# Product-key experts of a two-layer encoder step on one core: decode tokens by row gathers, dense stages 512 columns wide, sums kept in PSUM, low parts subtracted on VectorE

## The chip, the cores and the metric

One Trainium2 chip, one of its NeuronCores. The metric is device microseconds of one execution, the median of a few runs. The kernel before takes 5514.44 us (three runs, 5514.37 to 5516.7).

## What is computed

A two-layer encoder trunk over 512 prompt tokens and 32 decode tokens. Each layer is a mixer (RG-LRU and RWKV-7 side by side), then product-key expert retrieval, then a per-layer input embedding. Only the experts (`peer_ffn`) are changed:

```python
# per token: 8 heads, two half-queries each; u, v are (128*128, 1024)
q = (xb @ wq).reshape(PEER_BLOCK, PEER_HEADS, 2, PEER_HALF)
s = jnp.einsum('thsc,hskc->thsk', q, keys)            # 16 rows of 128 scores
top_s, top_i = lax.top_k(s, 16)
cand = top_s[:, :, 0, :, None] + top_s[:, :, 1, None, :]
best_s, best_c = lax.top_k(cand.reshape(PEER_BLOCK, PEER_HEADS, 256), 16)
e = (i1 * N_KEYS + i2).reshape(PEER_BLOCK, 128)       # 128 experts of each token
gate = softmax(best_s)
hid = jnp.einsum('td,tkd->tk', xb, jnp.take(u, e, axis=0))
wgt = gate * gelu(hid)
out = jnp.einsum('tk,tkd->td', wgt, jnp.take(v, e, axis=0))
```

## The kernel before

The program is written in five instruction streams (SyncE for loads, GpSimd, TensorE, ScalarE, VectorE) that meet at semaphores; each stream runs in the order in which it is written. SyncE, ScalarE and GpSimd also issue DMAs, in their own order.

The experts are computed densely: for each of 128 tiles of 128 experts, all 544 tokens are multiplied with all of them, and a gate matrix with zeros for the experts a token did not choose weighs the result. To keep float32 accuracy at the speed of float32r, each operand is cut into a high part (a copy rounded to float32r) and a low part (the rest), and each product is three matmuls (high x high, high x low, low x high).

**Hidden stage** (`hidden`, line 749). For one tile of experts: load 128 x 1024 weights (`load_u`), ScalarE makes the high part (`high_u`, line 1020), GpSimd the low part (`low_u`, line 505), TensorE does 48 matmuls (8 slices x 3 products x 2 halves of 272 tokens), ScalarE applies gelu (line 1027) and stores the result to memory (`expert_inputs`). Tiles go in pairs over two slots.

**Routing** (`route`, VectorE) runs beside it in blocks of 128 tokens, and a fifth of the 32 decode tokens. TensorE makes a block's scores (`scores`, line 759), ScalarE copies them out of PSUM (line 1035), VectorE does two rounds of top-16 (`top16`: lines 1380 to 1390) and the look-up of the numbers (lines 1424 to 1428), TensorE turns the result (`turn`). So far 16 hidden tiles run beside it (`PAIRS_A`); I call this part A of a block. In part B (`PAIRS_B`, 12 tiles), VectorE builds one-hot matrices of 4 tokens at a time (line 1446), GpSimd multiplies one with the gates (`weigh`, line 511), TensorE multiplies them (`gates`, line 780: 4 matmuls of 128 columns), ScalarE copies the product into a staging tile (line 1050). Two such groups follow each hidden tile; eight more groups stand alone at the end of the block. Then ScalarE stores the block's 8 MB of gates (`save`).

**Expert stage** (line 820). In 32 steps of 4 tiles: values and both matrices are loaded, VectorE multiplies gates and gelus (line 1463), makes the high part of the values (line 1458) and the low part of the products (line 1467), ScalarE the high part of the products (line 1095), GpSimd the low part of the values (line 538), TensorE does 24 matmuls of 272 columns for each of 8 output slices, and VectorE adds each slice to the residual `h` (line 1128).

Everything else (mixer, projections, norms, embedding) is the same in both kernels.

## Time and profile before

| | us |
|---|---|
| median of 3 runs | 5514.44 |
| span of the profiled execution | 5514.9 |
| first layer, from the end of the first scores to the end of the hidden stage's hand-over | 797.0 to 1866 |
| first layer, expert stage | 1866 to 2652 |
| second layer, the same two | 3534.3 to 4603, 4603 to 5390 |

TensorE is busy 86% of the span, GpSimd 36%, VectorE 55%, ScalarE 23%. The profiled execution stands within 0.5 us of the median, so sums made against the one hold for the other. In the rows below times are microseconds from the span's start; an arrow in brackets names what the engine had waited for.

### The profile page before, as it was taken

The numbers are of one execution on the slowest core, as the hardware profiler recorded it, in microseconds if no ns is written. First come the engines' busy times: TensorE is split into PE (matmuls) and PEld (weight loads), VectorE is DVE, ScalarE is ACT, GpSimd is POOL, SyncE is SP. The second block draws the span as 40 slices with busy tenths as digits, with TensorE's granted clock in tenths as the row PEclk, the third lists the DMA queues.
The fourth block names the chain that finished last, engine by engine and source line by source line (L and its number), as shares of the span: only waits on it lengthen the run. The fifth ranks groups of instructions, "written<-read, shape, count | busy, mean of one in ns | idle before, by whom it ended". The sixth has DMA issues, their size and how long they took to land.

```text
span 5514.9 us, 102578 instructions
## 1 busy us (share of the span) xinstructions
PE 4748.2 (86%) x38750; PEld 4569.1 (83%) x38750; DVE 3056.5 (55%) x4779; ACT 1254.8 (23%) x1872; POOL 1997.2 (36%) x902
## 2 busy tenths in 40 slices
PE   7566689899898799999884757898998987999997
PEld 7465589899898799999783646898998987999996
DVE  3453325655746577777235541355657456777772
ACT  3321123333332111111123211233333321111101
POOL 4100125463554444444040002363645634444430
PEclk9776899999999899999997768999999998999999
DMA  3000133535435555555120001335344345555541
GB/s 97 26 1 3 43 120 120 156 110 162 150 116 154 152 175 176 174 182 174 56 72 16 1 3 57 127 116 160 122 146 151 118 146 161 183 177 173 177 153 58
DMA packets 488297, 642.85 MB, mean 117 GB/s; under 512 B 60160, under 2 KB 322848, under 8 KB 487200
## 3 DMA queue, kind: packets, MB, share of 16 engines
q1 hardware_dynamic: 286384, 489.77, 27.1%
q10 hardware_dynamic: 201584, 151.55, 8.9%
q8 instruction: 42, 0.69, 0.1%
q0 software_dynamic: 256, 0.59, 0.0%
q14 instruction: 31, 0.25, 0.0%
HBM read 487.47 MB, written 154.35 MB: 116 GB/s over the span
## 4 chain that ended last, share of the span: by engine, by line
issue 43%; PE 36%; POOL 13%; DVE 4%; ACT 2%; DVEq 1%; POOLq 1%; ACTq 0%; DMA 0%; SPq 0%
PE ps L749 12%; PE ps L820 9%; POOL m L538 5%; PE ps L589 5%; POOL m L511 4%; POOL m L505 2%; PE ps L597 2%; PE ps L562 1%; PE ps L780 1%; DVE m L1446 1%; POOL m L485 1%; PE ps L653 1%; PE ps L661 1%; PE ps L698 1%; POOL m L481 1%
## 5 line engine op out<-in xcount | busy, mean ns | idle before, releaser
L749 PE MATMUL ps<-m,m 128*128 128x272 f32 x12288 | 1602.7, 292 | 73.9 <-POOL m L505 48.8
L749 PEld LDWEIGHTS ps<-m,m 128*128 128x128 f32 x12288 | 1578.5, 191 | 79.7 <-issue 79.7
L820 PE MATMUL ps<-m,m 128*128 128x272 f32 x12288 | 1572.1, 290 | 60.9 <-DVE m L1467 56.4
L820 PEld LDWEIGHTS ps<-m,m 128*128 128x128 f32 x12288 | 1558.2, 189 | 74.7 <-DVE m L1467 52.2
L505 POOL TENSOR_TENSOR m<-m,m 128x1024 fp32r<-128x1024 f32 x256 | 673.6, 2632 | 1000.5 <-ACT m L1020 1000.4
L538 POOL TENSOR_TENSOR m<-m,m 128x1024 fp32r<-128x1024 f32 x256 | 689.6, 2703 | 888.3 <-DVE m L1458 888.3
L1446 DVE TENSOR_TENSOR m<-m,m 128x512 f32<-128x512 f32 x544 | 672.2, 1292 | 447.1 <-PE ps L780 247.4
L1128 DVE TENSOR_TENSOR m<-ps,m 128x544 f32<-128x544 f32 (+1 forms) x528 | 378.9, 718 | 453.3 <-PE ps L820 340.4
L1463 DVE TENSOR_TENSOR m<-m,m 128x544 f32<-128x544 f32 x256 | 548.2, 2141 | 72.7 <-DMA m<-expert_inputs 40.9
L589 PE MATMUL ps<-m,m 128*128 128x272 f32 x3648 | 462.0, 289 | 87.3 <-POOL m L485 87.3
L589 PEld LDWEIGHTS ps<-m,m 128*128 128x128 f32 x3648 | 461.3, 191 | 88.9 <-issue 88.9
L1095 ACT ACTIVATE m<-m 128x544 fp32r<-128x544 f32 x256 | 168.8, 659 | 1407.8 <-DVE m L1463 1407.8
L511 POOL TENSOR_TENSOR m<-m,m 128x512 f32<-128x512 f32 x272 | 386.6, 1434 | 93.9 <-DVE m L1446 93.9
L780 PE MATMUL ps<-m,m 128*128 128x128 f32 x2176 | 317.2, 302 | 86.0 <-POOL m L511 85.6
L780 PEld LDWEIGHTS ps<-m,m 128*128 128x128 f32 x2176 | 290.2, 212 | 104.8 <-POOL m L511 104.4
L1027 ACT ACTIVATE m<-ps 128x544 f32<-128x544 f32 x256 | 160.0, 625 | 929.1 <-PE ps L749 827.3
L562 PE MATMUL ps<-m,m 128*128 128x272 f32 x1152 | 273.4, 401 | 77.4 <-DVEq L1364 56.0
L562 PEld LDWEIGHTS ps<-m,m 128*128 128x128 f32 x1152 | 224.2, 195 | 126.7 <-DVEq L1364 56.9
L485 POOL TENSOR_TENSOR m<-m,m 128x1024 fp32r<-128x1024 f32 x76 | 194.9, 2566 | 247.9 <-ACT m L875 247.9
L1020 ACT ACTIVATE m<-m 128x1024 fp32r<-128x1024 f32 x256 | 268.6, 1050 | 1.2 <-ACT m L1004 1.2
L496 POOL DMA_DIRECT2D out_small<-m x2 | 1.3, 649 | 717.0 <-DVEq L1344 717.0
L1380 DVE MAX8 m<-m 128x8 f32<-128x128 f32 (+3 forms) x240 | 59.0, 321 | 344.3 <-ACT m L1035 343.6
(194 smaller groups left out, 3439.2 us busy)
## 6 DMA issues: line engine op xcount, KB each, us to landing
m<-in_ut SPq DMA_DIRECT2D x256, 512.0 KB, 3.3
m<-in_v SPq DMA_DIRECT2D x256, 512.0 KB, 3.7
expert_inputs<-m ACTq DMA_DIRECT2D x256, 272.0 KB, 2.0
m<-gate_matrix SPq DMA_DIRECT2D x256, 272.0 KB, 4.1
m<-expert_inputs SPq DMA_DIRECT2D x256, 272.0 KB, 4.7
gate_matrix<-m ACTq DMA_DIRECT2D x8, 8192.0 KB, 30.5
m<-in_w_in SPq DMA_DIRECT2D x44, 512.0 KB, 3.8
m<-in_wq SPq DMA_DIRECT2D x32, 512.0 KB, 4.1
```

Of the source, the lines that this page charges most:

```text
L505: tt(ul[j], uraw[j], uh[j].bitcast(F32), ALU.subtract).then_inc(ul_ready, 1)
L511: tt(oneB[:, k % 2], oneB[:, k % 2], gate.unsqueeze(2).to_broadcast([P, GT, P]), ALU.mult).then_inc(ab_ready, 1)
L538: tt(vl[half * EC + j], vraw[j % 2], vh[half * EC + j].bitcast(F32), ALU.subtract).then_inc(vl_ready, 1)
L562: last = mm(ps[:, bank + a, 0:HALF], wslot[:, slot, k, :], rhs[:, n, a * HALF:(a + 1) * HALF], start=(n == 0), stop=(n == len(ks) - 1))
L589: last = mm(ps[:, 2 * j + a, 0:HALF], lhs[j][:, k, :], rhs[:, k, a * HALF:(a + 1) * HALF], start=(k + w == 0), stop=(k == KD - 1 and w == 2))
L749: last = mm(ps[:, j * 2 + a, 0:HALF], lhs[j][:, k, :], rhs[:, k, a * HALF:(a + 1) * HALF], start=(k + w == 0), stop=(k == KD - 1 and w == 2))
L780: last = mm(ps[:, 5 + k % 2, j * P:(j + 1) * P], oneA[:, k % 2, j, :], oneB[:, k % 2, j, :], start=True, stop=True)
L820: last = mm(ps[:, 4 + m % 2 * 2 + a, 0:HALF], lhs[at][:, m * P:(m + 1) * P], rhs[at][:, a * HALF:(a + 1) * HALF], start=(j + w == 0), stop ...
L1020: av(uh[j], uraw[j], ACT.Copy).then_inc(uh_ready, 1)
L1128: return tt(cut(at, HALF), halves(bank, HALF), cut(at, HALF), ALU.add)
L1446: tt(hot[:, s], iota.unsqueeze(1).to_broadcast([P, GT, P]), number.unsqueeze(2).to_broadcast([P, GT, P]), ALU.is_equal).then_inc(hot_ready, 1)
L1463: tt(wf[j % 2], gf[j], gs[j], ALU.mult).then_inc(w_ready, 1)
```

## The change

- The 32 decode tokens leave the dense stages. They are routed first, beside the first 8 hidden tiles; GpSimd then gathers, in 64 indirect DMAs a layer, the rows of `u` and `v` of their 128 experts (32 tokens x 4 chosen experts, one row of 1024 on each partition, two buffers). VectorE does the dot products (`dot`) and the weighted sum (`gather_add`), and TensorE folds the four partial sums.
- The dense stages cover 512 tokens: a hidden tile is 24 matmuls of 512 columns instead of 48 of 272.
- In the expert stage the eight output slices stay in the eight PSUM banks over all 128 tiles, and are added to `h` once at the end.
- The weights of both stages go through one ring of four slots (`ring_raw`, `ring_hi`, `ring_lo`); the low part overwrites the raw one. ScalarE makes the high part of both stages (`high`), VectorE the low part (`low`); GpSimd no longer computes in these stages.
- One-hot matrices are made by `tensor_scalar` of 128 x 128, the gate folded in, 16 for a tile. Part A of a block is now 12 hidden tiles, part B 16, each with two gate groups; none stand alone.
- Within routing, `low` is called at points between the steps (`between`).

The core of the diff:

```diff
-PAIRS_A, PAIRS_B = 8, 6
+QUADS_DEC, QUADS_A, QUADS_B = 2, 3, 4
@@ SyncE
+                def load_u(m, j):
+                    sp_.wait_ge(ring_done, L * STEPS + m * RING + j + 1)
+                    sp_.dma_start(ring_raw[j], ut[...]).then_inc(ring_in[j], 16)
@@ GpSimd
-                            weigh(b, g, 2 * j)
-                            weigh(b, g, 2 * j + 1)
-                            low_u(b * PAIRS_N + g + (PAIRS_A + 1), j)
+                for n in range(2 * DOTS):
+                    if n >= ROWS:
+                        pool.wait_ge(row_used, L * (2 * DOTS) + n - ROWS + 1)
+                    pool.indirect_dma_start(rows[n % ROWS], None, (u if n < DOTS else v)..., ...)
@@ TensorE
-                    for a in range(2):
-                        for k in range(KD):
-                            for w, (lhs, rhs) in enumerate([(uh, xh), (uh, xl), (ul, xh)]):
+                    pe.wait_ge(ring_low, i + 1)
+                    pe.wait_ge(ge_out, L * NK + m * RING + j + 1)
+                    for k in range(KD):
+                        for w, (lhs, rhs) in enumerate([(ring_hi, xh), (ring_hi, xl), (ring_lo, xh)]):
+                            last = mm(ps[:, 4 + j % 2, :], lhs[j][:, k, :], rhs[:, k, 0:SEQ], ...)
@@ TensorE, part B
                             hidden(b * QUADS_N + g + (QUADS_DEC + QUADS_A), j)
                             gates(b, g, 2 * j)
                             gates(b, g, 2 * j + 1)
@@ ScalarE
+                def gelu(m, j):
+                    i = L * NK + m * RING + j
+                    act.wait_ge(ring_done, L * STEPS + m * RING + j + 1 + RING)
+                    av(ge[j % 2], ps[:, 4 + j % 2, :], ACT.Gelu_apprx_tanh).then_inc(ge_out, 1)
+                    high(m + (j + RING - 1) // RING, (j + RING - 1) % RING)
+                    act.dma_start(act_d[...], ge[j % 2]).then_inc(act_saved[j % 2], 16)
@@ VectorE
+                def low(m, j):
+                    dve.wait_ge(ring_high, L * STEPS + m * RING + j + 1)
+                    tt(ring_lo[j], ring_raw[j], ring_hi[j].bitcast(F32), ALU.subtract).then_inc(ring_low, 1)
+                def ahead(m, j):
+                    low(m + (j + RING - 1) // RING, (j + RING - 1) % RING)
@@ VectorE, part B
+                        for j in range(RING):
+                            ahead(at + QUADS_A + g, j)
+                            for k in range(2 * j, 2 * j + 2):
+                                dve.wait_ge(gmat_done, i + 1)
+                                for n in range(GT):
+                                    ts(oneB[:, k % 2, n, :], iota, selq[...], selq[...], ALU.is_equal, ALU.mult)
+                                    last = ts(oneA[:, k % 2, n, :], iota, selq[...], None, ALU.is_equal)
+                                last.then_inc(hot_ready, 1)
+                            if j % 2 == 1:
+                                dot(b, g, j // 2)
@@ VectorE, expert stage
+                    for j in range(RING):
+                        weigh(e, j)
+                        low(e + QUADS, j)
+                        low_w(e, j)
```

VectorE in part B, before: one turn of its loop, two gate groups. `m_130` and `m_129` are the two one-hot matrices; after `gmat_done` it waits for nothing.

```order
L1446 ISA [waits gmat_done]
L1446 TENSOR_TENSOR m_130<-m_53,m_117 128x512
L1446 ISA
L1446 TENSOR_TENSOR m_129<-m_53,m_117 128x512
L1443 REGISTER_ALU
L1446 ISA [waits gmat_done]
```

The same place in the change, the first rows of a tile; L1400 is `low`, `m_144` and `m_143` are the one-hot matrices, and `ring_high` is counted up by ScalarE's `high`.

```order
L1399 ISA
L1400 TENSOR_TENSOR m_112<-m_116,m_108 128x1024 [waits ring_high]
L1524 REGISTER_ALU
L1527 TENSOR_SCALAR m_144<-m_53,m_130 128x128 [waits gmat_done]
L1528 TENSOR_SCALAR m_143<-m_53,m_130 128x128
```

The subtraction that stood on GpSimd now stands on VectorE ahead of the one-hot matrices of the same tile.

ScalarE at the same place in the change, one tile: gelu is L1045, `high` of the tile three further on is L1038, the copies of the gate products are L1067.

```order
L1044 ISA [waits ring_done]
L1045 ACTIVATE m_122<-ps 128x512 [waits act_saved0]
L1037 ISA
L1038 ACTIVATE m_111<-m_119 128x1024 [waits ring_in3]
L1047 ISA
L1048 ISA [waits ge_out]
L1048 DMA expert_inputs<-m_122 128x512
L1066 ISA
L1067 ISA [waits gmat_done]
L1067 ACTIVATE m_124<-ps 128x128x4
```

As before, `high` stands behind the gelu of the running tile, which waits for that tile's last matmul (`ring_done`); new is that the rows of VectorE above wait for it.

VectorE in the expert stage of the change, one tile (L1547 gates times gelus, L1400 low part of the values, L1552 low part of the products):

```order
L1547 TENSOR_TENSOR m106_155<-m106_155,m98_147 128x512
L1399 REGISTER_ALU
L1400 TENSOR_TENSOR m64_113<-m68_117,m60_109 128x1024
L1551 REGISTER_ALU
L1552 TENSOR_TENSOR m102_151<-m106_155,m110_159 128x512
```

The additions to `h` and the high part of the values, which stood between such rows before, are gone.

## Rows read from the trace of the kernel before

**Rows 1.** The page, costliest group: xcount | busy us, mean ns | idle before.
```profile
L749 PE MATMUL ps<-m,m 128*128 128x272 f32 x12288 | 1602.7, 292 | 73.9 <-POOL m L505 48.8
```
**Rows 2.** Windows of both stages: length, busy PE, PEld, DVE, ACT, POOL, clock, DMA share, GB/s.
```profile
797.00:1866.00 1069.00, 961.54 (x7387) 948.11 (x7387) 623.35 (x1322) 337.67 (x449) 533.51 (x266) 0.94 0.43 135
1866.00:2652.00 786.00, 782.57 (x6132) 776.24 (x6132) 595.62 (x631) 82.42 (x125) 334.68 (x124) 1.00 0.50 170
```
**Rows 3.** Chain that ended last: start, us, line xcount (f32: two records a matmul).
```profile
1297.05 60.66 PE ps L749 x480
...
5409.08 76.00 PE ps L562 x320
```
**Rows 4.** Timeline, TensorE at the end of part B: start us, us, what.
```profile
1444.98 6.27 PE L749 MATMUL ps<-m,m 128*128 128x272 f32 x48
1451.09 1.95 PE L780 MATMUL ps<-m,m 128*128 128x128 f32 x16
1457.31 3.52 PE L780 MATMUL ps<-m,m 128*128 128x128 f32 x16 [4.26 <-POOL m L511]
```
**Rows 5.** Timeline, part B: from a tile's last matmul to the low part's start.
```profile
1357.79 6.28 PE L749 MATMUL ps<-m,m 128*128 128x272 f32 x48
...
1364.24 0.62 ACT L1027 ACTIVATE m<-ps 128x544 f32<-128x544 f32 x1 [4.54 <-PE ps L749]
...
1364.76 1.05 ACT L1020 ACTIVATE m<-m 128x1024 fp32r<-128x1024 f32 x1
...
1365.88 2.80 POOL L505 TENSOR_TENSOR m<-m,m 128x1024 fp32r<-128x1024 f32 x1
```
**Rows 6.** Timeline of VectorE, one routing of 128 tokens.
```profile
1251.27 3.20 DVE L1380 MAX8 m<-m 128x8 f32<-128x128 f32 x16 [9.36 <-ACT m L1035]
...
1270.88 2.28 DVE L1403 TENSOR_TENSOR m<-m 128x2048 f32<-128x2048 f32 x1
...
1289.19 0.22 DVE L1413 TENSOR_SCALAR m<-m 128x128 uint32<-128x128 uint32 x1
1289.33 0.22 DVE L1414 TENSOR_SCALAR m<-m 128x128 uint32<-128x128 uint32 x1
...
1289.99 2.29 DVE L1424 TENSOR_TENSOR m<-m,m 128x2048 f32<-128x2048 f32 x1
...
1297.08 2.29 DVE L1424 TENSOR_TENSOR m<-m,m 128x2048 f32<-128x2048 f32 x1
```
**Rows 7.** Timeline, expert stage, first step: VectorE with and without GpSimd beside it.
```profile
1853.72 0.72 DVE L1463 TENSOR_TENSOR m<-m,m 128x544 f32<-128x544 f32 x1 [18.44 <-DMA m<-expert_inputs]
...
1863.33 2.35 POOL L538 TENSOR_TENSOR m<-m,m 128x1024 fp32r<-128x1024 f32 x1 [1.90 <-DVE m L1458]
1863.35 2.92 DVE L1463 TENSOR_TENSOR m<-m,m 128x544 f32<-128x544 f32 x1
```
**Rows 8.** Windows of TensorE around a wait of 4.26 us: length, busy, granted clock, DMA, GB/s.
```profile
1456.00:1457.50 1.50, 0.20 (x1) 1.00 0.31 44
1457.50:1459.00 1.50, 1.50 (x9) 0.63 0.79 306
1459.00:1460.50 1.50, 1.50 (x8) 0.50 0.00 0
1460.50:1462.00 1.50, 1.04 (x8) 0.73 0.00 0
```
**Rows 9.** Timeline and waits of ScalarE's queue behind a store of gates.
```profile
1245.82 0.58 ACTq L1055 DMA_DIRECT2D gate_matrix<-m  x1
...
1261.74 10.95 ACTq L1031 DMA_DIRECT2D expert_inputs<-m  x1
```
**Rows 10.** Waits: who for whom, us in total, times, longest.
```profile
ACT m L1027 <- issue: 89.1, 8, 12.5
```
**Rows 11.** DMA issues: KB each, median us to landing.
```profile
m<-expert_inputs SPq DMA_DIRECT2D x256, 272.0 KB, 4.7
gate_matrix<-m ACTq DMA_DIRECT2D x8, 8192.0 KB, 30.5
```

More of the change, by code:

```diff
@@ L441, in _ @@
+                sp_.wait_ge(ring_done, L * STEPS + NK + RING)
+                passed(sp_)
+                for j in range(2, RING):
+                    load_gates(0, j)
+                    load_v(0, j)
                 for j in range(2):
@@ new lines, in _ @@
+                for j in range(RING):
+                    experts(0, j, first=(j == 0))
+                with pe.Fori(1, QUADS - 1) as e:
+                    for j in range(RING):
+                        experts(e, j)
+                for j in range(RING):
+                    experts(QUADS - 1, j, final=(j == RING - 1))
+                pe.wait_ge(bank_added, L + 1)
+                pe.wait_ge(dec_sum, L + 1)
+                passed(pe)
+                for k in range(KD):
+                    last = mm(ps[:, 0, k * DEC:(k + 1) * DEC], xdec[:, k * P:(k + 1) * P], fold, start=True, stop=True)
@@ L823, in _ @@
+                last.then_inc(fold_done, 1)
                 norm(L, 2)
@@ new lines, in gates, with save @@
+                    av(stage[:, :, bass.ds(g * (2 * RING * GT) + k * GT, GT)],
+                       ps[:, 6 + k % 2, :].rearrange("p (j n) -> p n j", j=GT), ACT.Copy).then_inc(gmat_out, 1)
+                def save(b, col):
+                    act.wait_ge(gmat_out, L * GROUPS + b * (BLK // GT) + BLK // GT + 2)
+                    act.dma_start(gate_d[:, :, col], stage[:, :, :]).then_inc(gate_saved, 16)
+                for j in range(RING - 1):
+                    high(0, j)
+                scores(L * NBLK, DEC, s2_dec)
@@ L1082, in _ @@
[L1082 to L1095 removed]
+                    save(b, bass.ds(b * BLK, BLK))
@@ L1096, in _ @@
+                high(QUADS, RING - 1)
+                high_w(0, RING - 1)
+                with act.Fori(1, QUADS) as e:
+                    for j in range(RING):
+                        high(e + QUADS, j)
+                        high_w(e, j)
                 norm(L * 3 + 3, 2)
@@ L1476, in step @@
-                def step(e, half):
-                    for m in range(KD):
-                        add(e, m)
-                        for make, j in prepare[m]:
-                            make(e + 1, 1 - half, j)
-                for part in prepare:
-                    for make, j in part:
-                        make(0, 0, j)
-                with dve.Fori(0, ESTEPS // 2 - 1) as e2:
-                    step(e2 * 2, 0)
-                    step(e2 * 2 + 1, 1)
-                step(ESTEPS - 2, 0)
@@ new lines, in _ @@
+                for j in range(RING - 1):
+                    low(0, j)
+                pace = Pace(0, QUADS_DEC * RING)
+                route(L * NBLK, DEC, s2_dec, pace).then_inc(sel_ready, 1)
+                dve.drain()
+                copy(dsel[0:DEC, 0, :], sel_t[0:DEC, 0, :])
+                stt(dsel[0:DEC, 1, :], sel_t[0:DEC, 1, :], float(NK), sel_t[0:DEC, 2, :], ALU.mult, ALU.add)
+                dve.drain()
+                ts(dsel[0:DEC, 1, :].bitcast(U32), dsel[0:DEC, 1, :], small_of("row", 0)[0:DEC], None, ALU.add).then_inc(dsel_ready, 1)
@@ new lines, in low_w, with gather_add @@
+                def low_w(e, j):
+                    dve.wait_ge(wh_ready, L * NK + e * RING + j + 1)
+                    tt(wtl[j], gf[j], wth[j].bitcast(F32), ALU.subtract).then_inc(wl_ready, 1)
+                def gather_add(n, r, i):
+                    dve.drain()
+                    dve.wait_ge(row_in[r], L * (16 * DOTS) + 8 * DOTS + 16 * n + 16)
+                    stt(xdec, rows[r], dw[:, i], xdec, ALU.mult, ALU.add).then_inc(row_used, 1)
+                for j in range(RING):
+                    weigh(0, j)
+                    low(QUADS, j)
+                    low_w(0, j)
```

553 lines of the change are left out of this document (286 added, 267 removed).

## The prediction, on record before the changed kernel ran

> **What bounds the kernel now.** I read four views in this order. The page's costliest group shows the engine that sets the time: the hidden stage's matmuls cover 1602.7 us, with 73.9 us of waits before them [rows 1]. The windows of the two stages show where it is continuous: in the hidden stage TensorE is busy 961.5 of 1069 us at a mean clock of 0.94, in the expert stage 782.6 of 786 us at 1.00 [rows 2]. Both layers are alike to 1 us (the table), so I work out one layer and double it. The expert stage is bound by TensorE alone. The hidden stage is nearly so, less about 107 us at block boundaries. So the number of columns is what must get cheaper, and what matters beside it is whether the smaller engines still stay out of TensorE's way. The third view, the timeline of one tile in part B, answers that for now: a tile's 48 matmuls start at 1444.98, the gate matmuls behind them at 1451.09 (6.11 us), with no wait between [rows 4]. The fourth is routing on VectorE [rows 6].
>
> **The change part by part, for one layer.**
>
> *Wider matmuls.* 480 matmuls of 272 columns take 60.66 us, 126.4 ns each, where 272 columns at 2.4 GHz are 113.3 ns: 13 ns over. 320 records of two 272-column passes take 237.5 ns each for 226.7 ns: 11 ns over [rows 3]. The surplus goes with the instruction rather than with the column, so I take 213.3 + 11.2 = 224.5 ns for 512 columns, 5.39 us for a tile of 24 instead of 6.07 us for 48. Bounds: 215 ns (surplus almost gone) and 238 ns (surplus per column). Expert stage: 3072 x 0.2245 = 690 us instead of 786, **-96**. The range for it is 660 to 731.
>
> The Trainium skill, "TensorE: Matmul & The Clock Gate" (Part 2, "Back-to-back issue gap"), gives columns over 2.4 GHz plus 2.5 ns a matmul for a warm array, 215.7 ns here. Our row has 13 ns of surplus and not 2.5, and I keep to the row; by the page's rule the sum would be some 75 us lower over both layers.
>
> *Expert stage beside TensorE.* VectorE now does for each tile one product and two subtractions. A 544-element one takes 0.72 us when GpSimd is idle and 2.92 us beside it [rows 7], and a 2048-element one 2.28 us [rows 6], so 512 elements are 0.7 us and 1024 are 1.22 us: 2.6 us a tile, and a quarter of a weighted row sum (1.3 us). That is 3 us in 5.39. Loads start when TensorE has finished the slot, three tiles ahead (16 us); they land in 5 us [rows 11] and need some 4 us more of ScalarE and VectorE. Covered by 7 us, cost nothing; with slower loads this cover goes first. The end is new: eight additions out of PSUM of 0.7 us each, a fold on TensorE and one more addition, 9 us where one of 0.7 us was, **+8**, bounds 6 and 12.
>
> *Part A.* Routing a block costs VectorE, by start times: 1251.27 to 1270.88 for the first top-16, to 1289.99 for the sums and the second, 7.1 us for each of two look-ups and 1 us of tail [rows 6]: 53.9 us. Ten `low` of 1.22 us stand in it now, 66 us, against 12 tiles of 5.39 = 64.7 us on TensorE. VectorE thus becomes the bound there by a little. It also waits: each `low` waits for a `high` behind the gelu of the tile three before it, and behind each store of gates ScalarE's queue stands still for 11 us, from 1261.74 on, 27 us after the store in all [rows 9]; this happens 8 times in the program [rows 10], once for each store. So `low` of the fifth tile comes about 24 us after the scores, 13.5 us late, and I get 2 + 66 + 2 + 13.5 + 1 = 84.9 us from scores to turn. The old part A took 1357.5 - 1249 = 108 us, for 16 tiles. The decode tokens' own routing runs beside 8 tiles (43 us) but takes 70 us, and the first block's can only begin behind it: its turn comes at 137.1 us, where 20 tiles and scores are 112.
>
> *Part B, the step on which it hangs.* In VectorE's order `low` of tile i+3 stands ahead of the one-hot matrices of tile i, and it waits for ScalarE's `high` of tile i+3, which stands behind the gelu of tile i, which waits for the last matmul of tile i. The gate matmuls of tile i follow directly on that matmul and wait for the one-hot matrices. What was parallel is now one chain, in each of 64 tiles. From the rows: last matmul ends at 1364.07, gelu starts 0.17 later, `high` 0.52 after that and lasts 1.05, so it is done at 1365.81, 1.74 us after the matmul; the next engine starts 0.07 later [rows 5]. Then `low` 1.22 us and eight `tensor_scalar` at 0.14 us from start to start [rows 6], 1.12 us. TensorE gets its first group 4.2 us after its last matmul; the second is another 1.2 us behind. The gate matmuls take 0.97 us a group, half of the 1.95 us for 16 records at full clock [rows 4]. The tile takes 5.39 + 4.25 + 0.97 + 0.2 + 0.97 = 11.8 us.
> And the clock: after the 4.26 us wait the granted clock goes to 0.5, and 16 records take 3.52 us [rows 4, 8]. The same wait of 3.8 to 4.3 us stands once in each of the five blocks, and 0.5 follows each time. In the new part B such a wait stands in each tile. I add 1.6 us (both groups at 1.2 GHz, the hidden tile again at 2.4 GHz): 13.3 us a tile. Bounds: 11.8 (the clock holds) and 15.0 (the half clock reaches on into the hidden tile), and 0.9 us more if a `tensor_scalar` with scalars from memory takes 0.2 us. A tile with its two groups takes 7.81 us before (6.11 + 1.7) and the change would need 7.3 without the chain.
>
> *The other edits.* The gate groups that stood alone at a block's end are gone; that is in the sum below, as is the old hand-over to the expert stage (about 28 us without matmuls), of which 4 us remain, since gates are stored eight tiles earlier. The replication of decode tokens and its transposes lie beside GpSimd's low parts of the norm. A gather of 512 KB has no row; the nearest are 4.7 us for 272 KB and 30.5 us for 8 MB in small pieces [rows 11]. I take 5 us. VectorE asks for one each two tiles (26 us) or each four (21.6 us), so it is hidden; bounds 0 and 30.5 us, and see the rivals.
>
> *The sum.* After the first turn at 137.1 us: part B 16 x 13.3 - 1 = 212; three blocks of 4.5 (scores) + 84.9 + 211.5 = 301 each, 903; the last 8 tiles with a stall behind the store, 55. Hidden stage 1307 us, hand-over 4, expert stage 690, end 9: 2010 us. Before: 1069 + 786 = 1855. So **+155 us a layer, +310 in all**: 5514.9 + 310 = **5825 us**. The median before is 0.5 us below the profiled execution, which changes nothing.
>
> **Rivals.**
> *The chain does not form (faster).* If the one-hot matrices were ready when the hidden tile ends, a tile would take 7.3 us and the hidden stage 1307 - 64 x 6.0 = 923 us: 229 us less a layer than before, about 5055 us. It decides at 10.9 us a tile: below that the kernel gets faster (155 / 64 = 2.4 us under 13.3). For it: in the old timeline TensorE never waits there [rows 4]. Against it: the orders of both engines, and every wait in them. 7%.
> *The chain, with all else at its good end (faster).* Full clock in part B (-96 a layer), 215 ns a matmul (-38), no still stand of ScalarE's queue (-45): about 5465 us. Against it: five of five waits and eight of eight stores. 5%.
> *Gathers set the pace (slower still).* One at a time at 30.5 us, the expert stage would be 32 x 30.5 = 976 us, +286 a layer, with the hidden stage as forecast: about 6400 us. For it: GpSimd must make the descriptors and no row shows that. 4%.
> *The stores' stand and the chain as forecast, but the half clock longer.* 15.0 us a tile: about 6040 us; part of the forecast's upper side.
>
> **How the numbers follow.** The chain with its clock: 84%, its times 5630 (clock holds) to 6040. With the matmul's bounds of -76 and +128 around the centre, and the two faster rivals left out, the range is 5600 to 6030. A difference of 0.2%, 11 us, is about what can be told from no change. Faster 0.12, same 0.01, slower 0.87.
>
> **What would show it.** In the profile after: waits of TensorE before the gate matmuls for VectorE's one-hot matrices, near 4.2 us each and 128 in number, the largest wait of the program; a granted clock near 0.5 behind them; VectorE waiting for ScalarE's `high` in part B; an expert stage of 690 us a layer without waits; 224 ns a matmul. It would be wrong if those waits were short, or if matmuls of 512 columns came much below 215 ns, or if TensorE waited in the expert stage for a gather.

## The result

The changed kernel takes **6161.9 us** (median of four runs, 6157.7 to 6162.5) against 5514.4 us before (four runs, 5514.3 to 5516.7): ratio 1.117, 95% interval 1.116 to 1.118. The forecast was 5825 us, range 5600 to 6030. The direction was right, and the time lies 337 us above the forecast and 132 us above the range.

The page of the changed kernel, costliest groups: busy us, mean ns, then the idle time ahead of them and what ended most of it. They answer to [rows 1].

```profile
L764 PE MATMUL ps<-m,m 128*128 128x512 f32 x6144 | 1558.8, 413 | 222.1 <-ACT m L1045 194.4
L823 PE MATMUL ps<-m,m 128*128 128x512 f32 x6144 | 1419.6, 393 | 17.5 <-DVE m L1552 17.5
L789 PE MATMUL ps<-m,m 128*128 128x128 f32 x2048 | 484.7, 427 | 608.6 <-DVE m L1528 608.6
```

L764 is the hidden stage, L823 the expert stage, L789 the gate matmuls. The expert stage has become what was wanted: 17.5 us of waits in the whole program. The gate matmuls now wait 608.6 us for VectorE's one-hot matrices (L1528), and 194.4 us of the hidden stage are waits for ScalarE's gelu (L1045). In the old kernel the gate matmuls waited 86.0 us in all, nearly all of it in the groups that stood alone at a block's end:

```profile
L780 PE MATMUL ps<-m,m 128*128 128x128 f32 x2176 | 317.2, 302 | 86.0 <-POOL m L511 85.6
```

The waits for VectorE, counted (us in total, times, longest):

```profile
PE ps L789 <- DVE m L1528: 608.6, 129, 4.8
DVE m L1400 <- ACT m L1038: 1672.8, 162, 106.3
```

129 waits of 4.7 us on average, for the 128 part B tiles of the program. The second row is the link behind it: VectorE's low part (L1400) waits for ScalarE's high part (L1038). One tile in the timeline (start, length, then in brackets the idle time ahead):

```profile
986.14 0.60 ACT L1045 ACTIVATE m<-ps 128x512 f32<-128x512 f32 x1 [4.88 <-PE ps L764]
...
986.64 1.05 ACT L1038 ACTIVATE m<-m 128x1024 fp32r<-128x1024 f32 x1
...
987.72 1.22 DVE L1400 TENSOR_TENSOR m<-m,m 128x1024 fp32r<-128x1024 f32 x1 [9.15 <-ACT m L1038]
988.86 0.34 DVE L1527 TENSOR_SCALAR m<-m,m 128x128 f32<-128x128 f32 x1
989.12 0.28 DVE L1528 TENSOR_SCALAR m<-m,m 128x128 f32<-128x128 f32 x1
989.31 0.34 DVE L1527 TENSOR_SCALAR m<-m,m 128x128 f32<-128x128 f32 x1
...
990.81 3.56 PE L789 MATMUL ps<-m,m 128*128 128x128 f32 x16 [4.70 <-DVE m L1528]
...
994.12 5.82 PE L764 MATMUL ps<-m,m 128*128 128x512 f32 x24
```

The hidden tile ends at 986.1; gelu, high part, low part and eight `tensor_scalar` follow one another, each on the heels of the last, and only then does TensorE get its gate matmuls, 4.7 us later. They take 3.56 us where 16 such records took 1.95 [rows 4]. In the other tiles of part B the hidden matmuls take 5.8 to 7.0 us, so the lower clock reaches into some of them (in the tile of 7.0 us the granted clock is still 0.50 from 1008.4 to 1010.0).

Windows of one part B and of the expert stage (length, TensorE busy, ..., granted clock, DMA share, GB/s) answer to [rows 2]:

```profile
934.68:1168.00 233.32, 157.22 (x642) 131.58 (x643) 89.75 (x294) 43.65 (x64) 6.55 (x7) 0.82 0.25 76
2252.70:2964.00 711.30, 709.48 (x3072) 578.25 (x3072) 350.88 (x417) 212.86 (x252) 28.10 (x30) 1.00 0.60 205
```

Part B: 16 tiles in 233 us, 14.6 us each, at a clock of 0.82. The expert stage runs through at 1.00: 709.5 us for 3072 matmuls, 231 ns each.

Part A of a later block, timeline: the queue of ScalarE behind the store of gates, answering to [rows 9].

```profile
1168.21 3.74 PE L772 MATMUL ps<-m,m 128*128 128x128 f32 x32
1169.35 0.68 ACTq L1072 DMA_DIRECT2D gate_matrix<-m  x1
...
1179.82 31.96 ACTq L1048 DMA_DIRECT2D expert_inputs<-m  x1
...
1272.93 0.52 PE L780 MATMUL ps<-m,m 128*128 128x128 f32 x3 [3.43 <-DVE m L1474]
```

The next store of expert inputs is handed over 10.5 us after the store of gates and stands for 32 us; before it stood for 11. The store itself has become slower: 42.5 us to landing in the median of the eight (39.6 to 45.4; this one 45.4) for 30.5. DMA issues of the page (KB, us to landing) and the stand of ScalarE as a wait (total, times, longest), answering to [rows 10, 11]:

```profile
gate_matrix<-m ACTq DMA_DIRECT2D x8, 8192.0 KB, 42.5
...
ACT m L1045 <- issue: 237.6, 8, 32.8
```

One layer against the sum of the prediction, from scores on:

| | forecast, us | measured, us | difference |
|---|---|---|---|
| to the first turn | 137.1 | 136.8 | 0 |
| first part B (16 tiles) | 212 | 233.5 | +21.5 |
| three blocks (scores, A, B) | 3 x 301 | 3 x 335.6 | +104 |
| last 8 tiles | 55 | 69.4 | +14 |
| hand-over to the experts | 4 | 8.3 | +4 |
| expert stage | 690 | 709.5 | +20 |
| its end | 9 | 10.1 | +1 |

Part A, from the end of the scores to the turn, takes 101.0, 98.2 and 97.3 us in the three blocks, where 84.9 was forecast. The differences come to 165 us a layer, 330 of the 337 us.

### The profile page after: what moved, and what is told of

Same layout as the page of the kernel before. It is cut to its first block, busy times and chain, and to the rows that moved or that the text cites. A ratio compares the mean times of both kernels' runs of the same rounds, so it can differ in the third digit from the quotient of the medians.

```text
span 6160.1 us, 75206 instructions
## 1 busy us (share of the span) xinstructions
PE 4729.2 (77%) x26376; PEld 3960.2 (64%) x26376; DVE 2716.1 (44%) x6287; ACT 1475.0 (24%) x2076; POOL 376.4 (6%) x254
## 4 chain that ended last, share of the span: by engine, by line
PE 60%; DVE 16%; issue 13%; ACTq 4%; ACT 4%; DVEq 1%; DMA 1%; POOL 1%; SPq 0%; POOLq 0%
PE ps L823 22%; PE ps L764 15%; PE ps L789 8%; PE ps L598 7%; ACTq L1048 4%; ACT m L1038 2%; DVE m L1527 2%; DVE m L1528 2%; DVE m L1400 2%; PE ps L606 1%; PE ps L571 1%; DVE m L1427 1%; DVE m L1420 1%; DVE m L1415 1%; DVE m L1424 1%
## 5 line engine op out<-in xcount | busy, mean ns | idle before, releaser
L764 PE MATMUL ps<-m,m 128*128 128x512 f32 x6144 | 1558.8, 413 | 222.1 <-ACT m L1045 194.4
L764 PEld LDWEIGHTS ps<-m,m 128*128 128x128 f32 x6144 | 1210.9, 200 | 517.9 <-ACT m L1045 212.4
L823 PE MATMUL ps<-m,m 128*128 128x512 f32 x6144 | 1419.6, 393 | 17.5 <-DVE m L1552 17.5
L1400 DVE TENSOR_TENSOR m<-m,m 128x1024 fp32r<-128x1024 f32 x512 | 624.2, 1221 | 1683.6 <-ACT m L1038 1672.8
L823 PEld LDWEIGHTS ps<-m,m 128*128 128x128 f32 x6144 | 1157.0, 188 | 280.1 <-DVE m L1552 18.4
L789 PE MATMUL ps<-m,m 128*128 128x128 f32 x2048 | 484.7, 427 | 608.6 <-DVE m L1528 608.6
L789 PEld LDWEIGHTS ps<-m,m 128*128 128x128 f32 x2048 | 443.8, 320 | 673.2 <-DVE m L1528 670.1
L1038 ACT ACTIVATE m<-m 128x1024 fp32r<-128x1024 f32 x512 | 539.8, 1055 | 753.5 <-DMA m<-in_v 725.2
L598 PE MATMUL ps<-m,m 128*128 128x272 f32 x3648 | 461.0, 289 | 53.1 <-POOL m L519 53.1
L598 PEld LDWEIGHTS ps<-m,m 128*128 128x128 f32 x3648 | 460.3, 190 | 54.6 <-issue 54.6
L1547 DVE TENSOR_TENSOR m<-m,m 128x512 f32<-128x512 f32 x256 | 177.1, 692 | 680.7 <-DMA m<-expert_inputs 680.3
L1045 ACT ACTIVATE m<-ps 128x512 f32<-128x512 f32 x256 | 152.8, 597 | 1258.3 <-PE ps L764 1004.0
L1067 ACT ACTIVATE m<-ps 128x512 f32 x256 | 152.9, 597 | 827.8 <-PE ps L789 827.8
L1527 DVE TENSOR_SCALAR m<-m,m 128x128 f32<-128x128 f32 x1024 | 346.6, 339 | 0.0
L571 PE MATMUL ps<-m,m 128*128 128x272 f32 x1152 | 273.4, 401 | 77.4 <-DVEq L1380 56.0
L571 PEld LDWEIGHTS ps<-m,m 128*128 128x128 f32 x1152 | 224.3, 195 | 126.6 <-DVEq L1380 56.9
L1528 DVE TENSOR_SCALAR m<-m,m 128x128 f32<-128x128 f32 x1024 | 284.6, 278 | 0.0
L1104 ACT ACTIVATE m<-m 128x512 fp32r<-128x512 f32 x256 | 162.1, 633 | 250.5 <-DVE m L1547 250.5
L519 POOL TENSOR_TENSOR m<-m,m 128x1024 fp32r<-128x1024 f32 x76 | 194.4, 2560 | 256.3 <-ACT m L892 256.3
## 6 DMA issues: line engine op xcount, KB each, us to landing
gate_matrix<-m ACTq DMA_DIRECT2D x8, 8192.0 KB, 42.5
```

The lines of the kernel that those rows point to most:

```text
L519: tt(dst[j], wslot[:, j, 0:KD, :], high[j].bitcast(F32), ALU.subtract).then_inc(low_ready, 1)
L571: last = mm(ps[:, bank + a, 0:HALF], wslot[:, slot, k, :], rhs[:, n, a * HALF:(a + 1) * HALF], start=(n == 0), stop=(n == len(ks) - 1))
L598: last = mm(ps[:, 2 * j + a, 0:HALF], lhs[j][:, k, :], rhs[:, k, a * HALF:(a + 1) * HALF], start=(k + w == 0), stop=(k == KD - 1 and w == 2))
L764: last = mm(ps[:, 4 + j % 2, :], lhs[j][:, k, :], rhs[:, k, 0:SEQ], start=(k + w == 0), stop=(k == KD - 1 and w == 2))
L789: last = mm(ps[:, 6 + k % 2, j * P:(j + 1) * P], oneA[:, k % 2, j, :], oneB[:, k % 2, j, :], start=True, stop=True)
L823: last = mm(ps[:, m, :], lhs[j][:, m, :], rhs[j], start=(first and n == 0), stop=(final and n == 2))
```

## The experiments

The theory going in: the chain is what makes the kernel slower; what was mis-sized is the chain's own length, the store of gates, and the surplus of a wide matmul. Each run was compared with the kernel before on the same chip, whose medians there were 5511.6 to 5513.2 us.

**1. The chain cut on VectorE.** `ahead` (the low part of tile i+3) goes behind the tile's one-hot matrices:

```diff
                         for j in range(RING):
-                            ahead(at + QUADS_A + g, j)
                             for k in range(2 * j, 2 * j + 2):
...
                                 last.then_inc(hot_ready, 1)
+                            ahead(at + QUADS_A + g, j)
                             if j % 2 == 1:
```

> One edit: in part B the low part of the tile three ahead (and what goes with it) stands behind the one-hot matrices of the tile on VectorE, not ahead of them. The work is the same. Chain theory: the one-hot matrices are then made while TensorE is on the hidden tile, TensorE's waits of 4.7 us before the gate matmuls go, and so does the half clock behind them; a part B tile takes 5.5 + 1.95 + 0.3 = 7.8 us instead of 14.6, 16 of them 125 us instead of 233, over eight blocks 870 us less: 5290 us (5230 to 5380), faster than the kernel before. Rival (VectorE's sheer work, not its order: one low part 1.22, sixteen tensor_scalar 3.7, half a dot product 0.8, drains): VectorE stays the bound, the waits shrink by at most 1 to 2 us a tile, 5900 to 6050 us. Third: TensorE's wait goes but the pace moves to the loads (3.8 us to landing, three tiles ahead): waits for the low part at the start of hidden tiles, 5400 to 5600 us.

Measured: 5287.8 us (5278.7 to 5289.7), ratio 0.959 (0.957 to 0.960). That is 874 us less than the changed kernel, and faster than the kernel before. Part B in the timeline of TensorE, and the window over it:

```profile
949.68 5.81 PE L764 MATMUL ps<-m,m 128*128 128x512 f32 x24
955.33 1.95 PE L789 MATMUL ps<-m,m 128*128 128x128 f32 x16
957.03 5.82 PE L764 MATMUL ps<-m,m 128*128 128x512 f32 x24
```

```profile
945.00:1050.00 105.00, 104.25 (x564) 88.67 (x563) 77.60 (x259) 35.79 (x56) 6.57 (x7) 1.00 0.51 150
```

A tile takes 7.35 us from start to start instead of 14.6, TensorE is busy 104.25 of 105 us, and the clock is 1.00. The same instructions on the same engines, in another order, are worth 874 us. So VectorE's work was never the bound. The rival on the work falls. So does the one on loads: hidden tiles in part B start without a wait.

**2. The chain cut on ScalarE.** VectorE's order stays; the high part of tile i+3 stands ahead of the gelu and of its waits:

```diff
                     i = L * NK + m * RING + j
+                    high(m + (j + RING - 1) // RING, (j + RING - 1) % RING)
                     act.wait_ge(ring_done, L * STEPS + m * RING + j + 1 + RING)
...
                     av(ge[j % 2], ps[:, 4 + j % 2, :], ACT.Gelu_apprx_tanh).then_inc(ge_out, 1)
-                    high(m + (j + RING - 1) // RING, (j + RING - 1) % RING)
```

> One edit, at the other end of the chain: on ScalarE the high part of the tile three ahead is made ahead of the gelu of the tile (and of its wait for the last matmul), not behind it; VectorE's order stays. Chain theory: the chain is cut as well, but the high part now comes 3.8 us (load) + 1.05 after the tile before has ended, the low part 1.22 and the first one-hot group 1.8 us later, that is 7.9 us against 1.95 + 5.5 = 7.4 us of TensorE: waits of about 0.5 to 1.5 us, 8.3 to 9 us a tile, 5330 to 5500 us. Rival (VectorE's work is the bound): no more than 1 us a tile, 6000 us or more.

Measured: 5373.5 us (5371.5 to 5375.6), ratio 0.975 (0.973 to 0.977). TensorE in part B:

```profile
983.45 5.81 PE L764 MATMUL ps<-m,m 128*128 128x512 f32 x24
989.09 1.05 PE L789 MATMUL ps<-m,m 128*128 128x128 f32 x8
990.76 1.16 PE L789 MATMUL ps<-m,m 128*128 128x128 f32 x8 [0.62 <-DVE m L1528]
991.68 5.82 PE L764 MATMUL ps<-m,m 128*128 128x512 f32 x24
```

8.2 us a tile, with waits of about 0.6 us for VectorE, as expected. Either cut does it. What both have in common is that no step between a tile's last matmul and its gate matmuls depends on that last matmul. The chain is shown.

**3. The clock, taken by itself.** The expectation rests on my first reading of the trace, that 2.3 of the 14.6 us were the half clock. Eighteen matmuls without use fill the wait:

```diff
                             hidden(b * QUADS_N + g + (QUADS_DEC + QUADS_A), j)
+                            for f in range(18):
+                                mm(ps[:, 3, :], xh[:, 0, 0:P], xh[:, f % KD, 0:SEQ], start=True, stop=True)
                             gates(b, g, 2 * j)
```

> The changed kernel as it is, with 18 matmuls of 512 columns of no use (4.2 us) between each hidden tile of part B and its first gate matmuls, into a bank that nobody reads then; they fill most of TensorE's wait of 4.7 us. Clock theory (2.3 us of each part B tile are the half clock behind the wait): TensorE is busy through, the granted clock of part B goes from 0.82 to about 1.00, the 16 gate records take 1.95 us instead of 3.7, a tile 12.0 to 12.6 us instead of 14.6: 5830 to 5930 us, faster with more work. Rival (the clock costs nothing that the chain doesn't already set: what TensorE loses it would wait for anyway, or the half clock comes for another reason): 6140 to 6180 us. Worse, if the matmuls of no use run at the half clock themselves and take 8 us: over 6400 us.

Measured: 6019.2 us (6011.4 to 6023.1), ratio 1.092 (1.090 to 1.094): 143 us faster with 2304 more matmuls, but 90 us above the range of the clock theory. TensorE's timeline, then the windows from 1000 to 1100 us of this kernel and of the changed one:

```profile
953.29 5.80 PE L764 MATMUL ps<-m,m 128*128 128x512 f32 x24
958.93 4.31 PE L807 MATMUL ps<-m 128*128 128x512 f32 x18
963.79 1.16 PE L789 MATMUL ps<-m,m 128*128 128x128 f32 x8 [0.55 <-DVE m L1530]
965.60 1.16 PE L789 MATMUL ps<-m,m 128*128 128x128 f32 x8 [0.65 <-DVE m L1530]
966.52 5.81 PE L764 MATMUL ps<-m,m 128*128 128x512 f32 x24
```

```profile
1000.00:1100.00 100.00, 89.88 (x439) 72.11 (x438) 43.80 (x146) 20.51 (x31) 2.80 (x3) 1.00 0.26 79
```

```profile
1000.00:1100.00 100.00, 66.74 (x272) 56.25 (x273) 37.58 (x126) 19.14 (x28) 2.81 (x3) 0.81 0.24 71
```

The granted clock goes from 0.81 to 1.00, and a tile takes 13.3 us (15 tiles, 945.56 to 1145.00), where the same 15 tiles of the changed kernel take 14.5 each (947.49 to 1164.75). So the half clock costs 1.2 us a tile, not 2.3; the 143 us over 128 tiles say 1.1. The rest is the chain at full clock, and it can be read here term by term: hidden tile 5.64, to the first gate group 4.86, to the second 1.81, to the next tile 0.92. The second group waits 0.65 us for its eight `tensor_scalar` even at full clock. In the changed kernel part of the slow first group lay over that wait. That fits with a clock that costs less than its records show.

**4. The row pitch of the two buffers in DRAM.**

```diff
-        act_d = nc.dram_tensor("expert_inputs", [P, NK, SEQ], F32, kind="Internal").ap()
+        act_d = nc.dram_tensor("expert_inputs", [P, NK, T], F32, kind="Internal").ap()[:, :, 0:SEQ]
-        gate_d = nc.dram_tensor("gate_matrix", [P, NK, SEQ], F32, kind="Internal").ap()
+        gate_d = nc.dram_tensor("gate_matrix", [P, NK, T], F32, kind="Internal").ap()[:, :, 0:SEQ]
```

> One edit: the two DRAM buffers (gates and expert inputs) keep rows of 544 numbers, 2176 bytes from row to row as in the kernel before, of which 512 are used; nothing else changes. Pitch theory: the 8 MB store of gates is slower (42.5 us to landing against 30.5) because the rows lie 2048 bytes apart; with 2176 it lands in about 30 us, ScalarE's queue stands still for 11 us rather than 28 to 33, part A of three blocks takes 85 us instead of 101: 6040 to 6080 us. Rival (the store shares the DMA engines with more traffic: 512 KB loads, gathers and stores of expert inputs at a time when the old kernel had less): nothing changes, 42 us and 32 us stay, 6150 to 6165 us.

Measured: 6103.6 us (6102.7 to 6106.1), ratio 1.107 (1.105 to 1.109): 58 us less than the changed kernel, 24 us above the range of the pitch theory. Landing and stand:

```profile
gate_matrix<-m ACTq DMA_DIRECT2D x8, 8192.0 KB, 34.9
...
ACT m L1045 <- issue: 177.7, 8, 25.4
```

And the DMA rates in equal slices while the store runs, first the changed kernel (1168 to 1214 us), then this one (1168 to 1204):

```profile
GB/s 7 32 125 364 330 161 188 263 158 135 109 112 205 286 252 277 227 247 366 321 138 164 234 373 341 337 199 196 285 336 220 261 315 322 236 279 272 194 285 265
```

```profile
GB/s 0 5 91 282 340 348 346 321 316 317 313 316 316 315 220 236 408 349 345 344 320 369 368 339 333 323 318 323 409 338 339 325 317 317 319 315 316 316 352 336
```

In the changed kernel the rate moves between 109 and 373 GB/s; here it stands at 313 to 350 in most slices. So the layout of the buffers is a cause, for 7.6 of the 12 us by which the store had become slower. The other 4.4 us are there with the old distances too. In this window 11.0 MB move, with one gather of 0.5 MB and three loads of weights, where before 9.5 MB moved in 31 us.

The edit changes two distances at once, though: rows 2176 instead of 2048 bytes apart, and partitions (128 rows each) 272 instead of 256 KiB. Two more runs take them apart.

**5. Which distance.** On the changed kernel as it is, the same for both buffers. First only the partitions' distance, 260 KiB, with rows 2048 bytes apart:

```diff
-        gate_d = nc.dram_tensor("gate_matrix", [P, NK, SEQ], ...).ap()
+        gate_d = nc.dram_tensor("gate_matrix", [P, NK * SEQ + 1024], ...).ap()[:, 0:NK * SEQ].rearrange("p (k t) -> p k t", t=SEQ)
```

> The changed kernel with the two DRAM buffers padded by 4 KiB behind each partition's 128 rows: rows stay 2048 bytes apart, partitions are 260 KiB apart instead of 256. The run with rows of 544 numbers changed two distances at once (rows 2176 bytes apart instead of 2048, partitions 272 KiB instead of 256) and brought the landing of the store from 42.5 to 34.9 us. If the distance between partitions is what counts (128 streams in step, each a power of two from the next), this run lands in about 35 us and takes about 6104 us. If the distance between rows counts, it stays at 42.5 us and 6162. If both count, in between.

Then only the rows' distance, 2176 bytes, with partitions a power of two apart again (512 KiB):

```diff
-        gate_d = nc.dram_tensor("gate_matrix", [P, NK, SEQ], ...).ap()
+        gate_d = nc.dram_tensor("gate_matrix", [P, 131072], ...).ap()[:, 0:NK * T].rearrange("p (k t) -> p k t", t=T)[:, :, 0:SEQ]
```

> The counterpart: rows 2176 bytes apart, partitions 512 KiB apart, a power of two again. Partition theory: 42.5 us to landing or more, 6160 us or more. Row theory: 34.9 us and 6104 us. The Trainium skill, "DMA: Bandwidth & Descriptors" ("Latency and other measured facts"), has full rate for another kind of copy (16 KiB a partition) at 512 KiB between partitions and a loss only from 2 MiB on; by it neither this run nor the one before would differ from the other, and the partition theory would fall.

Measured: 6104.0 us (6099.6 to 6104.4) and 6104.4 us (6102.0 to 6106.2), both ratio 1.107 to 1.108 and both like run 4. The landing of the store in the first and in the second:

```profile
gate_matrix<-m ACTq DMA_DIRECT2D x8, 8192.0 KB, 34.1
```

```profile
gate_matrix<-m ACTq DMA_DIRECT2D x8, 8192.0 KB, 34.8
```

Each theory alone falls, since each was to hold in one of the two runs only. To take either distance off its power of two is enough; the store is slow only where both are, 2048 bytes and 256 KiB. The sizes also shift where the buffers lie, and both buffers were changed together; neither was tested apart. The Trainium skill, "DMA: Bandwidth & Descriptors" ("Latency and other measured facts"), reports copies that slow down at large powers of two between partitions, from 2 MiB on, and nearly full rate at 512 KiB (207 of 214 GB/s). The second run agrees as far as it goes: no loss at 512 KiB, with rows of 2176 bytes. The changed kernel does not agree: it loses at 256 KiB, with rows 2048 bytes apart.

**6. The order and the pitch together** (the edits of 1 and 4).

> Both edits of the two runs before: low part behind the one-hot matrices, and rows 2176 bytes apart. If they are independent, the time is that of the first less what the second saves: about 5290 - 110 = 5180 us under the chain and the pitch theory; 5290 if the pitch does nothing. A store that falls beside a faster part A may also cost more, not less: then the stall of ScalarE's queue (28 to 33 us) is seen in full as a wait of TensorE, and this run lies at or above the first.

Measured: 5218.7 us (5214.8 to 5219.5), ratio 0.946 (0.945 to 0.948); 5180 was expected, with 110 us for the pitch. It is worth 69 us on top of the first edit and 58 us without it. They are nearly independent, and the shorter part B does not cover the store. The wait of the hidden stage for ScalarE that is left (141.6 us) is mostly the stand of the queue; without that stand, in run 7, 14.1 us remain:

```profile
L764 PE MATMUL ps<-m,m 128*128 128x512 f32 x6144 | 1509.7, 404 | 168.6 <-ACT m L1045 141.6 <-DVE m L1400 26.6
```

**7. The store in pieces,** on top of the kernel of 6. Eight stores of 16 experts' rows each, one behind each gelu, in place of one store:

```diff
-                def save(b, col):
+                def save(b, i, col):
                     act.wait_ge(gmat_out, ...)
-                    act.dma_start(gate_d[:, :, col], stage[:, :, :]).then_inc(gate_saved, 16)
+                    rows = bass.ds(i * (NK // PIECES), NK // PIECES)
+                    act.dma_start(gate_d[:, rows, col], stage[:, rows, :]).then_inc(gate_saved, 16)
...
                             gelu(b * QUADS_N + g + QUADS_DEC, j)
+                            if before is not None:
+                                save(before, g * RING + j, bass.ds(before * BLK, BLK))
```

> On top of the kernel with both edits: the 8 MB store of a block's gates is issued as eight stores of 1 MB, one behind the gelu of each of the next eight hidden tiles (the last block's: two behind each of four). Queue theory: ScalarE's queue stands still because one store fills it and the next store of expert inputs can only be handed over when nearly all of it has landed (stand = landing time less the 10.5 us to the next store, less about 3: 42.5 - 10.5 = 32.0 for 31.96 measured, 34.9 - 10.5 - 3 = 21.4 for 21.85). 1 MB pieces at 316 GB/s take 3.3 us, less than a tile, so no stand is left: TensorE's 141.6 us of waits for the gelu go, 5218.7 - 110 to 140 = 5080 to 5110 us. Rival (the same bytes take the same time wherever they stand, and the loads pay for them: 1 MB + 0.5 MB + 0.25 MB in a tile of 5.65 us is 317 GB/s, all that a store reached): waits for the low part at the start of the tiles instead, 5180 to 5260 us.

Measured: **5076.6 us** (5072.0 to 5083.7), ratio 0.922 (0.920 to 0.923): the fastest kernel of the study, 142 us under that of 6 (a little more than the 110 to 140 expected) and 7.9% under the kernel before. The next block's scores and part A in TensorE's timeline, the window while pieces are stored, and the waits for the queue:

```profile
1056.13 3.74 PE L773 MATMUL ps<-m,m 128*128 128x128 f32 x32
1059.62 55.97 PE L765 MATMUL ps<-m,m 128*128 128x512 f32 x240
1115.86 5.83 PE L765 MATMUL ps<-m,m 128*128 128x512 f32 x24 [0.27 <-ACT m L1046]
1122.78 5.83 PE L765 MATMUL ps<-m,m 128*128 128x512 f32 x24 [1.09 <-DVE m L1409]
1132.03 0.52 PE L781 MATMUL ps<-m,m 128*128 128x128 f32 x3 [3.42 <-DVE m L1483]
```

```profile
1066.00:1110.00 44.00, 44.00 (x191) 35.56 (x190) 40.00 (x177) 13.24 (x17) 0.00 (x0) 1.00 1.07 320
```

```profile
ACT m L1046 <- issue: 47.7, 8, 8.8
```

Ten tiles run without a wait while the DMA engines move 320 GB/s, so the loads pay nothing for the store. The 47.7 us of waits for the queue all stand behind the last block of each layer, where two pieces are handed over behind each gelu; with one piece a tile there is no stand. Scores to turn is 1059.8 to 1132.0, 72 us.

The same kernel with the pitch of the changed kernel again (the edit of 4 undone):

> The fastest kernel so far (order, row pitch, store in pieces; 5076.6 us) with the pitch of the changed kernel again (rows 2048 bytes, partitions 256 KiB apart). If the pitch only acts by the stand of the queue, it is worth nothing once no stand is left: 5070 to 5090 us. If the slower store now takes bandwidth from the loads (1 MB pieces at 200 to 230 GB/s take 4.5 to 5 us of each 5.6 us tile, with 0.75 MB of other transfers), waits come back: 5100 to 5150 us.

Measured: 5079.2 us (5073.4 to 5083.9), ratio 0.922 (0.920 to 0.923), no difference to 5076.6. The pieces land in 7.0 us here and in 7.1 there (medians of 64), so in pieces of 1 MB this layout isn't slower at all; that it acts only by way of the queue is therefore not shown. Who stores in pieces needs no padding here.

**8. The gathers.** All but two of a layer's 64 gathers (124 of the program's 128, not 60 of 64 as the expectation has it) are replaced by 4 KB transfers, on the changed kernel as it is; the decode tokens' expert part is left out of the result.

```diff
+                    if n >= ROWS:
+                        pool.dma_start(rows[n % ROWS][:, 0:8], spare_d[0]).then_inc(row_in[n % ROWS], 16)
+                        continue
...
-                    stt(rows[r], rows[r], 1.0, xdec, ALU.mult, ALU.mult, accum_out=dhid[...]).then_inc(row_used, 1)
+                    stt(rows[r], rows[r], 1.0, xdec, ALU.mult, ALU.min, accum_out=dhid[...]).then_inc(row_used, 1)
```

> The changed kernel without 60 of its 64 gathers a program pair (all but the first two of a layer): 4 KB transfers with the same semaphores stand in their place, so the decode tokens' expert part is left out of the result; VectorE's products stay (with a minimum in place of a product). Hidden theory: the gathers cost nothing on the path, the chain stays, 6145 to 6165 us. Rival for the store: the gather of 0.5 MB that lies beside each store of gates is what slows it; then landing goes from 42.5 to about 40 us, ScalarE's queue stands 2 us less, 8 times: up to 20 us less, 6140. If the gathers set a pace anywhere, over 40 us less: under 6120 us.

Measured: 6149.5 us (6138.9 to 6151.8), ratio 1.116 (1.114 to 1.118), whose interval overlaps that of the changed kernel, though each of its four runs is below each of the other's (6157.7 to 6162.5). What moves in the trace is the store:

```profile
gate_matrix<-m ACTq DMA_DIRECT2D x8, 8192.0 KB, 40.4
...
ACT m L1048 <- issue: 218.0, 8, 29.4
```

The store lands in 40.4 us, 2.1 less, and the stand is 20 us shorter in all. By the medians the gathers cost 12 us, too little for the two intervals to tell from nothing; by the trace they cost the store 2.1 us (median of eight, 38.2 to 41.3 here and 39.6 to 45.4 with the gathers), about half of the 4.4 us that the layout left open, if the two causes add. The other half was not tested by itself; an additional load of weights lies in the same window.

**9. The price of a column,** a single run, on top of the kernel of 6. The hidden stage runs over 256 columns and the expert stage over 384; the rest of the dense output is left out.

```diff
-                            last = mm(ps[:, 4 + j % 2, :], lhs[j][:, k, :], rhs[:, k, 0:SEQ],
+                            last = mm(ps[:, 4 + j % 2, 0:256], lhs[j][:, k, :], rhs[:, k, 0:256],
...
-                            last = mm(ps[:, m, :], lhs[j][:, m, :], rhs[j],
+                            last = mm(ps[:, m, 0:384], lhs[j][:, m, :], rhs[j][:, 0:384],
```

> On top of the kernel with both edits: the hidden stage's matmuls run over 256 of the 512 columns and the expert stage's over 384 (half and a quarter of the dense outputs are left out); everything else stays. It prices the surplus of a matmul over its columns at 2.4 GHz (17.7 ns at 512 columns in the expert stage, 13 at 272 in the kernel before). If the surplus goes with the instruction: 384 columns take 177.7 ns, 256 take 124.4. If it goes with the column (0.0346 ns each): 173.3 and 115.5. In between, by the two measured points (7.9 ns + 0.0192 ns a column): 175.3 and 119.5. Expert stage 532 to 546 us instead of 710 if no load sets its pace (512 KB of weights and 512 KB of gates and inputs every 4.2 us is 250 GB/s).

Measured: the expert stage is busy 1073.4 us, and stretches of 120 and 72 hidden matmuls at full clock take 14.53 and 8.81 us:

```profile
L823 PE MATMUL ps<-m,m 128*128 128x384 f32 x6144 | 1073.4, 337 | 18.0 <-DVE m L1552 18.0
```

```profile
798.30 14.53 PE L764 MATMUL ps<-m,m 128*128 128x256 f32 x120
...
1038.38 8.81 PE L764 MATMUL ps<-m,m 128*128 128x256 f32 x72
```

The same stage in the kernel of 6:

```profile
799.66 44.84 PE L764 MATMUL ps<-m,m 128*128 128x512 f32 x192
...
847.84 16.96 PE L764 MATMUL ps<-m,m 128*128 128x512 f32 x72
```

Expert stage: 1073.4 / 6144 = 174.7 ns at 384 columns, 1419.2 / 6144 = 231.0 at 512, that is 0.440 ns a column and 5.8 ns besides. Hidden stage: a stretch ends about 0.25 us after its last start, so I take the difference of two stretches: (14.53 - 8.81) / 48 = 119.2 ns at 256 columns and (44.84 - 16.96) / 120 = 232.3 at 512, that is 0.442 ns a column and 6 ns besides. The kernel before fits as well: 0.44 x 272 + 6 = 125.7 for 126.4 [rows 3]. A column thus takes 0.44 ns and not the 0.417 of 2.4 GHz. Of the 17.7 ns of surplus at 512 columns two thirds grow with the columns. The value between the two pure theories was the nearest (175.3 and 119.5 expected).

## Why the prediction was wrong, and where it was right

**The chain in part B** (right in kind, too short by 1.2 us a tile). The forecast had 11.8 us at full clock and 1.6 for the clock. Run 3 gives 13.3 and 1.2. So the step that failed is the length of the chain, and in it two terms, with a third that goes the other way:
- `tensor_scalar` at 0.14 us. The row used was one on integers with constants [rows 6]. Those of the one-hot matrices are float32 and read their scalars from memory (which of the two counts wasn't tested), and in the tile shown above they start 0.26 and 0.19 us apart: 1.8 us for eight instead of 1.1. It counts twice, ahead of the first group (4.86 us in run 3 for 4.25) and between the groups (1.81 for 1.17). The prediction had named this as a bound of 0.9 us. It should have been the value, since the row it took was of another form.
- the hidden tile, 5.64 us for 5.39.
- the clock, 1.2 for 1.6, which goes the other way.

The first tile of a block is about 2 us longer than the others. 16 tiles, four blocks: 21.5 us a block, 172 us over both layers. This is half of the miss.

The range failed too. Its upper end, 6030 us, lies under the 6040 that the prediction itself has for the longer half clock alone. The 0.9 us a tile for `tensor_scalar` (115 us over 128 tiles) and the 128 us for the wide matmul were named but not added to it.

**Part A and the stand of the queue** (12 to 16 us in each of three blocks, and 14 us in the last eight tiles: 107 us over both layers). The steps of VectorE were right: without the stand the forecast is 84.9 - 13.5 = 71.4 us (its terms as written add to 84.5, not 84.9), and run 7, which has no stand there, takes 72. The step that failed is the stand, taken over from the kernel before as 11 us. In the traces it ends when the store has all but landed, 2 to 4 us before: the store shown above lands after 45.4 us, the next one is handed over at 10.5 and stands for 31.96, so 2.9 us remain. Before, 30.5 - 15.9 - 10.95 leaves 3.6 [rows 9, 11]; with the pitch of run 4, 34.9 - 10.5 - 21.85 leaves 2.6. Both terms, the landing and the time to the next store, moved. The store became slower by the layout of its buffer (7.6 us) and by more traffic beside it (4.4 us, of it 2.1 the gathers by run 8), and the next store came 5.4 us earlier. Some 3.5 us of that are TensorE's start on the next hidden tile, 2.4 us after the store for 5.9 before, where it waited for ScalarE's copy of the scores; the other 2 us are the tile itself, up to its gelu.

```profile
1251.69 19.89 PE L749 MATMUL ps<-m,m 128*128 128x272 f32 x144 [2.48 <-ACT m L1035]
```

The prediction read the length of a symptom and not the two times that make it.

**The wide matmul** (231 ns for 224.5). The step that failed is that the surplus goes with the instruction. Two counts at the same column number could not tell that, and run 9 does: 0.44 ns a column and about 6 ns besides. 20 us a layer in the expert stage, and 0.25 us in each hidden tile. The Trainium skill, "TensorE: Matmul & The Clock Gate" (Part 2, "Back-to-back issue gap"), has 215.7 ns at 512 columns for the isolated gap. The trace does not agree for this kernel, where a weight load goes with each matmul: 231.0.

**What was right.** The first turn at 136.8 us for 137.1. The expert stage without waits for loads or gathers (17.5 us of waits, all at its start). The gathers hidden but for what little they cost the store (run 8). The end of the expert stage, 10.1 for 9. The first rival, that the chain doesn't form, was priced at 5055 us, and run 1, in which it is cut, takes 5288. Of the 233 us between them 211 go when the store is mended (runs 6 and 7, 5077 us). That this comes so near to 5055 is in part luck: the rival kept a stand of 11 us that run 7 hasn't, and had the matmul at 224.5 ns.

**The other rivals.** No gather sets a pace. The longer half clock came in part: it reaches into some hidden tiles (5.8 to 7.0 us), but all of it together costs 1.2 us a tile, less than the 1.6 of the forecast. The 14.5 us a tile, near that rival's 15.0, come from the chain at full clock.

## What to carry to other kernels

When an instruction moves to another engine, follow for each waiting instruction behind it what it now depends on: here one subtraction ahead of independent work tied that work to the end of the tile, and the same instructions in the other order were worth 14% of the time. The stand of a queue behind a large store ended here 2 to 4 us before that store had landed, in every kernel that stored at once: work out the landing and the time until the next issue anew for the changed kernel, and issue a large store in pieces between the small ones. Take a duration from a row of the same form, operands included, or let the far bound be the value.

## What the runs showed of the hardware that was not expected

- **Two powers of two in DRAM.** A store of 8 MB in pieces of 512 bytes lands in 42.5 us (median of eight) with rows 2048 bytes and partitions 256 KiB apart, and in 34.1 to 34.9 us when either distance is another (2048 bytes with 260 KiB, 2176 bytes with 512 KiB or 272 KiB). In pieces of 1 MB there is no such difference, 7.0 and 7.1 us.
- **More work, less time.** 18 matmuls without use in each wait of 4.7 us keep the granted clock at 1.00 instead of 0.81 (both from 1000 to 1100 us) and make the program 143 us faster.
- **A column takes 0.44 ns** at a granted clock of 1.00, between 256, 384 and 512 columns, with 6 ns an instruction besides (from three column counts in two stages).
- **`tensor_scalar` with scalars from memory** on 128x128 takes 0.19 to 0.20 us from start to start with one such scalar and 0.26 us with two.
